# A modulation row copied before ScalarE's wait for the convolution, and the first body's modulation steps from the middle of its second tile

## What is computed

```python
mod = (jax.nn.silu(c) @ p['w_ada'] + p['b_ada'])[:, None, :]
sh_a, sc_a, g_a, sh_c, sc_c, g_c = jnp.split(mod, 6, axis=-1)
h = rmsnorm(x, p['norm_mix_g']) * (1.0 + sc_a) + sh_a
z = h @ p['w_in']
z_a = z[..., :A_SHIFT_COLS]
z_qk = z[..., A_SHIFT_COLS:A_SHIFT_COLS + B_QK_COLS]
...
qk = lax.conv_general_dilated(zp, p['b_conv_w'][:, None, :].astype(zp.dtype), (1,), 'VALID', ...) + p['b_conv_b']
qk = jax.nn.silu(qk.astype(f32))
```

## Time and profile before

| what | value |
|---|---|
| three timed runs | 2782.35 us median, 2781.85 to 2787.63 |
| the profiled execution, its own time | 2783.28 us |
| its span | 2781.5 us |
| mean granted TensorE clock | 0.963 of full speed |
| TensorE matmul busy | 2624.6 us, 94% of the span |
| GpSimd, VectorE, ScalarE busy | 63%, 47%, 35% |
| stretch of the first two bodies | 118.6 to 190.9 us of the span |

### The profile page before, as it was taken

How to read it: one execution, slowest core, us unless ns; L and a number is a source line. 1 busy time by engine, 2 the same in 40 slices (tenths; PEclk the granted TensorE clock), 3 DMA queues, 4 the chain that set the end, 5 groups by cost and what they waited for, 6 DMA issues and landing times.

```text
span 2781.5 us, 59271 instructions
## 1 busy us (share of the span) xinstructions
PE 2624.6 (94%) x24297; PEld 2422.5 (87%) x24297; DVE 1314.1 (47%) x2316; ACT 964.2 (35%) x1388; POOL 1757.1 (63%) x790
## 2 busy tenths in 40 slices
PE   5799999888979999999999999999999999999997
PEld 3689999657757999999999988999889999888886
DVE  0450256773236456993677365101554004555456
ACT  1233433241223434444343333333333333322233
POOL 0256677012225776888555799777988777778763
PEclk6899999879988999999999999999999999999998
DMA  9968754577864443445554655555655557788862
GB/s 378 333 242 278 267 184 164 186 259 239 256 229 155 168 165 121 164 156 173 181 179 175 193 182 196 188 184 178 199 184 187 186 187 254 247 294 300 283 243 109
DMA packets 179856, 587.50 MB, mean 211 GB/s; under 512 B 28008, under 2 KB 37880, under 8 KB 150904
## 3 DMA queue, kind: packets, MB, share of 16 engines
q1 hardware_dynamic: 137104, 506.63, 52.8%
q0 software_dynamic: 14672, 55.59, 5.5%
q10 hardware_dynamic: 27928, 23.07, 2.7%
HBM read 558.78 MB, written 26.46 MB: 210 GB/s over the span
## 4 chain that ended last, share of the span: by engine, by line
PE 38%; POOL 31%; issue 23%; DMA 4%; DVE 3%; ACT 1%; POOLq 0%; SPq 0%; ACTq 0%; DVEq 0%
PE bank L876 37%; POOL ring_lo L755 24%; DMA kept<-in_w_ada 3%; POOL ring_lo L831 3%; POOL staged L852 3%; POOL staged L845 1%; DMA staged<-late_acts,staged 1%; DVE staged L2167 1%; PE bank L879 0%; DMA staged<-in_w_ada 0%; ACT staged L1658 0%; DVE staged L2291 0%; POOLq L754 0%; ACT staged L1661 0%; ACT hi_peer L1661 0%
## 5 line engine op out<-in xcount | busy, mean ns | idle before, releaser
L755 POOL TENSOR_TENSOR ring_lo<-kept,hi_peer 128x1024 fp32r<-128x1024 f32 x416 | 1050.3, 2546 | 318.9 <-ACT hi_peer L1661 318.2
L1661 ACT ACTIVATE hi_peer<-kept 128x1024 fp32r<-128x1024 f32 x544 | 546.1, 1051 | 1100.4 <-PE bank L876 1100.3
L876 PE MATMUL bank<-h_hi,ring_lo 128*128 128x288 f32 x2848 | 840.1, 295 | 0.0
L876 PE MATMUL bank<-act_hl,hi_peer 128*128 128x248 f32 (+1 forms) x3072 | 708.6, 316 | 23.6 <-POOL ring_lo L831 16.7
L876 PE MATMUL bank<-h_hi,hi_peer 128*128 128x288 f32 x2048 | 609.1, 297 | 5.3 <-POOL ring_lo L755 2.6
L876 PE MATMUL bank<-h_lo,hi_peer 128*128 128x288 f32 x2048 | 604.2, 295 | 0.0
L876 PEld LDWEIGHTS bank<-act_hl,hi_peer 128*128 128x128 f32 x3072 | 502.8, 189 | 84.2 <-POOL ring_lo L831 24.1
L876 PE MATMUL bank<-act_hl,ring_lo 128*128 128x248 f32 x2048 | 566.0, 276 | 0.0
L876 PEld LDWEIGHTS bank<-h_hi,ring_lo 128*128 128x128 f32 x2848 | 538.1, 189 | 0.0
L876 PE MATMUL bank<-staged 64*64 64x64 f32 (+11 forms) x6600 | 372.4, 283 | 37.4 <-issue 19.2
L755 POOL TENSOR_TENSOR ring_lo<-kept,hi_front 128x1024 fp32r<-128x1024 f32 x100 | 243.7, 2459 | 240.5 <-ACT hi_front L1661 240.5
(11 more groups left out here) (261 smaller groups left out, 3111.3 us busy)
## 6 DMA issues: line engine op xcount, KB each, us to landing
kept<-in_peer_u SPq DMA_DIRECT2D x128, 1024.0 KB, 4.8
kept<-in_peer_v SPq DMA_DIRECT2D x128, 1024.0 KB, 5.7
kept<-in_w_ada SPq DMA_DIRECT2D x64, 1024.0 KB, 8.7
kept<-in_w_in SPq DMA_DIRECT2D x50, 1024.0 KB, 4.8
staged<-in_w_ada SPq DMA_DIRECT2D x32, 1024.0 KB, 6.3
kept<-in_w_adaf SPq DMA_DIRECT2D x32, 1024.0 KB, 5.5
kept<-in_w_out SPq DMA_DIRECT2D x16, 1024.0 KB, 4.8
kept<-in_w_q SPq DMA_DIRECT2D x16, 1024.0 KB, 4.8
```

Of the source, the lines that this page charges most:

```text
L755: pool.tensor_tensor(ring_lo[:, n % RING_SLOTS, cols], ring[n % RING_SLOTS][:, cols], hi_slot(n)[:, cols].bitcast(F32), ALU.subtract).then ...
L876: return pe.matmul(out, lhsT, rhs, start=start, stop=stop)
L1661: return act.activation(out, in_, ACT.Copy)
```

## The change

It has two parts. On ScalarE the copy of the modulation row (`early_take(i, 0)`) moves, in the two q/k bodies, from the head of the fourth tile to the end of the third tile's take, ahead of the wait for the convolution. On TensorE the first body gets an order of its own: steps 0 and 1 move from the middle and the end of tile 0 to the middle and the end of tile 1, steps 2 and 3 come in the middle and at the end of tile 2. The bodies after it are as they were. Nothing is added or removed.

```diff
-            def early_body(i, gates=False):
-
+            for j in range(4):
+                pe.wait_ge(S("z_free"), j + 1)
+                dense(n_z + j, h_hi, h_lo, 0, j % 2, "h", {1: 0, 2: 2}.get(j))
+                if j == 0:
+                    gate_part(3).then_inc(S("gates_ready"), 1)
+                elif j < 3:
+                    early_step(0, 2 * j - 1)
+            early_turn(0)
+            with pe.Fori(1, EARLY_BODIES) as i:
                 for j in range(4):
                     pe.wait_ge(S("z_free"), i * 4 + (j + 1))
                     dense(n_z + j, h_hi, h_lo, i, j % 2, "h", {0: 0, 2: 3}.get(j))
-                    if gates and j == 0:
-                        gate_part(3).then_inc(S("gates_ready"), 1)
                     if j < 2:
                         early_step(i, j + 1)
                 early_turn(i)
-
-            early_body(0, True)
-            with pe.Fori(1, EARLY_BODIES) as i:
-                early_body(i)
...
             with act.Fori(0, 2) as i:
                 for j in range(4):
-                    if j == 3:
-                        early_take(i, 0)
                     act.wait_ge(used, i * 4 + (n_z + j + 1))
...
                     copy(zqs[:, j % 2, :, 0:3],
                          conv0[:, bass.ds(i * 4 + j, 1)].rearrange("p o b t -> p (o b) t")).then_inc(S("zq_full"), 1)
+                    if j == 2:
+                        early_take(i, 0)
                     act.wait_ge(S("conv_ready"), i * 4 + (j + 1))
```

## The result

The changed kernel took 2767.28 us in the median of 8 runs (2757.16 to 2771.65), the kernel before 2782.27 us beside it (8 runs, 2773.6 to 2787.63). The ratio is 0.9949, with a 95% interval of 0.9939 to 0.996: faster, by 15.0 us. I had said 2772.0 and 2768.5 to 2777.5. The direction and the place were right, the size was not, and the range did not hold the time.

The account below looks back on a forecast made before the run. TensorE was taken as the bound, unbroken from 191.63 us, with removable waits before. Terms 2.45 + 2.01 + 4.65 + 2.13 made 11.24 us; 10.4 under the median was taken: 2772.0 us, range 2768.5 to 2777.5.

Parts of the forecast that it names:

- Each wait goes, none takes its place: TensorE, first bodies: walking the new order, all waits vanish with 0 to be paid back and 11.2 us gained.
- One of my own signs of being wrong: First body: a wait for `in_w_ada` in tile 2 would show the forecast wrong; no size given.
- The wait for step 0's weights: TensorE, tile 0 of the first body: the wait for step 0's modulation transfer goes, gaining 2.45 us.
- The turns: TensorE's first two turns of the modulation row: idle time waiting for ScalarE's copy goes, 2.01 and 2.64 us.
- The clock term: TensorE behind both turns: matmuls at the 1.2 GHz level after idle time, 1.5 us each, 3.0 together, would go.
- Step 2's weights: First body, tile 2: the transfer lands 5.5 us after issue, with 7.6 us available, so no wait, 2 us to spare.
- a pair that lands together: Step 2's and tile 4's transfers might land together, about 7.6 us after issue; the sum would be 10.7 to 11.2 us.
- ScalarE's own cycle: Second body: ScalarE needs 7.85 us a tile, TensorE wants 7.63; tile 8's low half still comes 1.8 us early.
- What is behind the Z stage moves alike: From 496 us on, everything starts from TensorE's last tile, so the whole gain carries through to the end.
- The landing time that would make the kernel slower: Modulation transfers in all bodies: landing times of about 11.4 us would make the kernel slower; rival's chance 4%.
- how the numbers follow: Whole kernel: forecast 70% (2769.5 to 2774 us), rivals 15%, 10% and 4%, a gain above 13 us 1%.
- the rival that spends the gain: Behind the Z stage: four more stretches at 1.2 GHz take 6 of 11 us, giving 2777 to 2786; chance 10%.

Follow-up runs that it names:

- The copy alone: Only ScalarE's copy of the modulation row moved, against the kernel before, TensorE's first-body steps left in place: 2773.84 us, ratio 0.9973.
- the spread steps: Changed kernel with first-body step 0 behind tile 0's gate part, step 1 mid tile 1, steps 2 and 3 mid and end of tile 2: 2766.87 us.
- the loop pair: Changed kernel plus a loop of 4 unused matmuls after the eighth body, run once or 21 times: means 2768.2 and 2778.8 us.

## Why the prediction was right or wrong

- **Each wait goes, none takes its place**: right but for one small wait. The copy is at 144.8 us and costs nothing; the turns come 32.6, 63.1 and 93.65 us after the start of tile 0, I had 33.1, 63.6 and 93.7. (My last one does not fit the two before it, which with bodies of 30.5 us lead to 94.1.) One of my own signs of being wrong came true in small: step 3, at the end of tile 2, waits 0.58 us for `in_w_ada`.
- **The wait for step 0's weights, 2.45 us**: right in place and about in size (2.28 to 3.02 us of idle time in the five profiles that have it). The copy alone leaves it, the steps' move takes it away.
- **The turns, 2.01 and 2.64 us**: right, and the same within 0.1 us in every profile of before.
- **The clock term, 3.0 us**: right in the one profile it was read from, wrong as a term with a size. The three profiles of before show it as about 3.0, 0 and 3.9 us. I took less than the whole of it for the point (10.4 us and not 11.2, the middle of my bounds), which was in the right direction for the mean and no help for the range.
- **Step 2's weights, "5.5 us, 2 us to spare"**: mis-sized. They landed after 7.0 us and just in time, step 3's after 8.1 us and 0.58 late. The issues, at 130.3 and 134.65 us, came 1.3 us behind steps 0 and 1, as I had them. The Trainium skill's remark (DMA: Bandwidth & Descriptors, Two DMAs through the same engine are not ordered), read by me as a pair that lands together after 7.6 us, was nearer in size than my row's 5.5, though the pair did not land together (137.3 and 139.8 us), and in one of the four profiles the 5.5 us came out. What I had missed is that four transfers of 1 MB now come within 5 us; that this is what slows them is likely, but not shown. With more room, as in the spread steps, there is no wait.
- **ScalarE's own cycle, 1.8 us to spare**: held. In the copy-only kernel and in the changed one nothing waits for `ring_lo` at tile 8.
- **What is behind the Z stage moves alike**: right on average within the error of 1.4 us (10.6 for 10.7 us in the loop pair), though in single executions its length differs by up to 11 us.
- **The landing time that would make the kernel slower, "about 11.4 us"**: a slip in the sum. With two steps at 7.6 us of room and fourteen at 10.7, the waits reach the 11.2 us won at 11.0. Nothing hangs on it.
- **The step that failed is how the numbers follow.** The range, "2768.5 to 2777.5", was built from the bounds of the terms alone. It put the scatter of the measured medians at nothing, without a reason, and left 1% for a gain above 13 us. I had three timed runs of before, 5.8 us apart, quoted them for the rival that spends the gain, and did not let the same scatter work downwards. The changed kernel's 20 single runs go from 2757 to 2775 us. By that a median of eight is good to about 2 us either way, and before's median of three to 2 or 3, so by my estimate a lower bound near 2766 was called for. The three groups of runs gave 15.0, 13.7 and 9.5 us for the same pair. Against the 12.4 us of all runs (2782.3 - 12.4 = 2769.9 us, inside my range) my point of 10.4 was low by 2.0. That the measured median lies outside the range is the draw of the first eight runs on top.

That the time to the third turn scatters by the clock is shown. For the 1.8 us between 10.6 and 12.4 I can't say more than that it is within the errors.

## What to carry to other kernels

A copy that another engine waits for belongs ahead of its own engine's next long wait, if its inputs are there: here that, and four moved steps, gave 12.4 us (with an error of 1.1) for no added instruction. Where one engine feeds another in a cycle, moving its work earlier also moves the feeder, so the value of a removed wait is found by walking both engines through the order, not from the wait's own row. And a term read from one execution, like a fall of the clock, is a chance and not a price: state it with the scatter of the timed runs, on both sides.

## What the runs showed of the hardware that I had not expected

- The same wait of 2.0 to 2.7 us on TensorE was followed by some 3.3 us at the 1.2 GHz level in one execution and by none in another of the same program.
- Four 1 MB transfers issued between 130.3 and 135.3 us landed 7.0, 8.8, 8.1 and 10.3 us after issue; one with 3.3 us to the next took 5.1. But in another execution of the same program the two modulation transfers among them took 5.5 and 6.9.
- 84 further matmuls in TensorE's straight code cost 11.4 us in place, and the kernels had 5 and 9 us more in the end. A stretch of 220 us much further on, in long straight code, became 7 to 10 us shorter, with the granted clock up from 0.92 to 0.95 and 0.96. The same work in a loop left that stretch as it was and cost its full time. What ties the place of the code to the clock is not shown.
